# A two-layer mixer and expert kernel: a third expert unit loaded ahead, requests in slot order, late norm rows, residual and gate products at other places of the PE stream

## The reference, cut to what matters

```python
h = _layernorm(DEEPNORM_ALPHA * h + mix, ln_mix_g[layer], ln_mix_b[layer])
ffn = _moe(h, w_router, b_router, moe_w_gate[layer], moe_w_up[layer], moe_w_down[layer])
h = _layernorm(DEEPNORM_ALPHA * h + ffn, ln_ffn_g[layer], ln_ffn_b[layer])
...
for e in range(N_EXPERTS):                       # inside _moe
    h = jax.nn.silu(xt @ w_gate[e]) * (xt @ w_up[e])
    y = y + combine[:, e:e + 1] * (h @ w_down[e]).astype(jnp.float32)
```

## Time and profile before

| | |
|---|---|
| median of 3 runs | 1013.69 us (1008.77 to 1015.44) |
| the profiled execution | 1008.44 us, its span 1006.5 us |
| PE busy | 959.6 us, 95% of the span |
| DVE, ACT, POOL busy | 298.7, 224.0, 15.2 us |
| DMA | 278.84 MB, mean 277 GB/s |
| experts of layer 0, of layer 1 | about 283 to 500 us, about 781 to 998 us |

### The profile page before, as it was taken

The page is one execution under the profiler, slowest core; times in us unless marked ns, Lnnn a source line. Parts: engine busy times, 40 slices in busy tenths (PEclk is TensorE's granted clock), DMA queues, the critical chain, the costliest instruction groups (busy, mean ns, idle before and its releaser), DMA issues.

```text
span 1006.5 us, 9999 instructions
## 1 busy us (share of the span) xinstructions
PE 959.6 (95%) x3984; PEld 512.8 (51%) x3984; DVE 298.7 (30%) x773; ACT 224.0 (22%) x466; POOL 15.2 (2%) x29
## 2 busy tenths in 40 slices
PE   8989999999999999989899999999998999999986
PEld 7644875554543335333385557888445334453321
DVE  4230162331521213120234433564316112121203
ACT  1120243221211112110211533431532111111101
POOL 2000000000000000000000000000000000000001
PEclk9999999999999999999999999999999999999999
DMA  8982424152789999999994423352555899999994
GB/s 274 335 316 85 160 92 167 43 209 83 302 327 388 422 421 421 421 419 422 398 386 143 168 84 124 127 210 82 210 209 218 323 406 421 421 421 421 418 419 165
DMA packets 65779, 278.84 MB, mean 277 GB/s; under 512 B 8852, under 2 KB 9216, under 8 KB 41920
## 3 DMA queue, kind: packets, MB, share of 16 engines
q1 hardware_dynamic: 63856, 271.60, 68.5%
q0 software_dynamic: 1872, 6.53, 1.9%
HBM read 277.04 MB, written 1.06 MB: 276 GB/s over the span
## 4 chain that ended last, share of the span: by engine, by line
PE 83%; DMA 11%; DVE 4%; ACT 1%; issue 1%; SPq 0%; DVEq 0%
PE bank L679 78%; DMA ring<-in_moe_w_up 10%; PE bank L1040 2%; DMA ring<-in_w_in_ab 1%; PE bank L1097 1%; PE bank L1045 1%; PE bank L1393 1%; PE bank L775 1%; ACT feat L1461 0%; PE bank L956 0%; DVE stat L2241 0%; ACT rstd L1461 0%; DVE feat L2223 0%; DVE hT L2248 0%; DVE h L2478 0%
## 5 line engine op out<-in xcount | busy, mean ns | idle before, releaser
L679 PE MATMUL bank<-ring,hT 128*64 128x512 f32 (+1 forms) x832 | 276.7, 597 | 8.9 <-DMA ring<-in_moe_w_up 4.1
L679 PE MATMUL bank<-ring,feat 128*64 128x512 f32 (+1 forms) x1152 | 226.3, 594 | 8.6 <-ACT feat L1461 4.1
L679 PEld LDWEIGHTS bank<-ring,hT 128*64 128x64 f32 (+1 forms) x832 | 109.8, 162 | 165.8 <-issue 157.8
L679 PE MATMUL bank<-hT,ring 128*128 128x256 f32 x768 | 168.4, 380 | 1.2 <-DMA ring<-in_w_in_ab 1.0
L679 PEld LDWEIGHTS bank<-hT,ring 128*128 128x128 f32 x768 | 145.8, 191 | 21.2 <-DMA ring<-in_w_in_ab 1.7
L679 PEld LDWEIGHTS bank<-ring,feat 128*64 128x64 f32 (+1 forms) x1152 | 74.3, 131 | 150.2 <-issue 140.8
L1461 ACT ACTIVATE feat<-bank 32x512 f32<-32x512 f32 (+3 forms) x128 | 61.1, 494 | 393.3 <-PE bank L679 251.3
L679 PE MATMUL bank<-ring,yT 128*128 128x512 f32 x256 | 112.8, 595 | 0.0
L2231 DVE COPY feat<-bank 32x512 f32<-32x512 f32 (+1 forms) x56 | 38.5, 687 | 150.4 <-PE bank L679 149.8
L679 PEld LDWEIGHTS bank<-ring,yT 128*128 128x128 f32 x256 | 47.8, 190 | 55.5 <-issue 54.6
L2223 DVE TENSOR_TENSOR feat<-feat,bank 128x512 f32<-128x512 f32 x16 | 11.0, 688 | 185.7 <-PE bank L679 185.7
(11 more groups left out here) (249 smaller groups left out, 549.9 us busy)
## 6 DMA issues: line engine op xcount, KB each, us to landing
ring<-in_moe_w_up SPq DMA_DIRECT2D x64, 1024.0 KB, 16.4
ring<-in_moe_w_gate SPq DMA_DIRECT2D x56, 1024.0 KB, 14.4
ring<-in_moe_w_down SPq DMA_DIRECT2D x56, 1024.0 KB, 13.0
ring<-in_w_in_ab SPq DMA_DIRECT2D x24, 1024.0 KB, 9.1
ring<-in_w_in_cd SPq DMA_DIRECT2D x24, 1024.0 KB, 12.7
ring<-in_w_out_ab SPq DMA_DIRECT2D x8, 1024.0 KB, 5.8
ring<-in_moe_w_down SPq DMA_DIRECT2D x16, 512.0 KB, 17.9
ring<-in_w_out_cd SPq DMA_DIRECT2D x8, 1024.0 KB, 6.1
```

The lines of the kernel that those rows point to most:

```text
L679: return nc.tensor.matmul(o, l, r, start=start, stop=stop)
```

## The change

1. **A third unit of pair 3 is loaded ahead**: up of its first expert. Its first half goes to `spare`, a tile that now holds `prob` and `gate_row`; its second half to `tok[:, 2]`, where the norm rows lie.
2. **The norm rows are loaded later**: for the norm after layer 0's experts POOL asks for them when the four result banks are done, for the last norm when up of layer 1's pair 3 is done. Before, both were asked for when h was normed after the mixer. DVE applies gain and bias to `h` (now `gained`) after its copies of cd0 and ahead of those of cd1.
3. **Requests in slot order**: SP asks for gate of pair 4 before up and down of pair 3. The skipped units leave slots that gate of pair 4 takes.
4. **Residual products** (`carry`) of token block 0 stand in routing, around `ranks` of block 1; those of block 1 in the two gaps of pair 7. The scatter of quad 0 into block 1's banks now starts the accumulation.
5. **Gate products**: gate uses bank 1. In pairs 0 and 1 the first chunk of the next pair's gate stands ahead of `hid_turn` and the second behind it (`AHEAD`), 4 of 16 products each time.
6. `weights_turn` stands between gate and up, into bank 2.
7. Of the eight pulls before pair 4, the last two now stand between chunks of pair 4's gate, as they do in pair 0.

```diff
@@ build @@
+AHEAD = (1, 2)
...
-        prob = sb("prob", [P, 2, CAUSAL])
-        gate_row = sb("gate_row", [16, 5, SEQ])
+        spare = sb("spare", [P, KC * FF // 2])
...
-        early = ((as_unit(yT[:, 0:8, :]), as_unit(yT[:, 8:16, :])), (as_unit(tok[:, 0, :, :]), as_unit(tok[:, 3, :, :])))
+        early = ((as_unit(yT[:, 0:8, :]), as_unit(yT[:, 8:16, :])), (as_unit(tok[:, 0, :, :]), as_unit(tok[:, 3, :, :])),
+                 (spare[:, :].rearrange("p (k n) -> p k n", n=FF), as_unit(tok[:, 2, :, :])))
...
-        first_pulls = ((0, 1, 0, 1), (2, 3, 0, 1))
+        first_pulls = ((0, 2, 0, 2), (1, 3, 0, 2))
+        second_pulls = ((0, 1, 2, 3), (1, 0, 2, 3))
@@ SP @@
                 fetch_early(1, 1)
+                fetch_early(2, 0)
...
                 fetch_early(0, 1)
-                for i in range(1, PAIRS - 1):
-                    stream_pair(i)
+                sp.wait_ge(h_ready, TB * (2 * layer + 1))
+                fetch_early(2, 1)
+                order = [(i, j) for i in range(1, PAIRS - 1) for j in (0, 2, 4)]
+                order.remove((EARLY_PAIR + 1, 0))
+                order.insert(order.index((EARLY_PAIR, 2)), (EARLY_PAIR + 1, 0))
+                for i, j in order:
+                    stream_part(i, j)
@@ POOL @@
-                if n % 2:
-                    pool.wait_ge(h_ready, TB * n)
+                if n == 1:
+                    for k in plan["ffn0"]:
+                        wait_ready(pool, "ffn0", k)
+                elif n == 3:
+                    wait_ready(pool, f"up1_{EARLY_PAIR // 2}{EARLY_PAIR % 2}", 3)
@@ PE, second_lists @@
                 pull(layer, 0, 0, 3)
+                carry(layer, 0, 0)
                 ranks(layer, 1)
+                carry(layer, 0, 1)
@@ PE, experts @@
+                def gate_chunks(at, ks):
+                    i, pair = divmod(at, 2)
+                    if ks[0] == 0:
+                        claim(f"gate{layer}_{i}{pair}", 1)
+                        held_w[at] = [weights(at, e, KC) for e in range(2)]
+                    for k in ks:
+                        for e in range(2):
+                            last = mm(bank[1][e * 2 * SLOTS:(e + 1) * 2 * SLOTS, :],
+                                      slots_of(xg[i % 2][:, k, :], pair, e), held_w[at][e](k), k == 0, k == KC - 1)
...
-                        for t in range(TB):
-                            for j in range(4):
-                                pull(layer, 1, t, j)
+                        for t, j in ((0, 0), (0, 1), (0, 2), (0, 3), (1, 0), (1, 1)):
+                            pull(layer, 1, t, j)
...
+                            gate_chunks(at, range(2 if at in AHEAD else 0, KC))
+                        if pair:
+                            claim(f"weigh{layer}_{i}", 2)
+                            pe.wait_ge(selw_ready, QUADS * layer + i + 1)
+                            weights_turn(2).then_inc(ready[2], 1)
...
-                        if i == 0:
-                            carry(pair, 0)
+                        if at + 1 in AHEAD:
+                            gate_chunks(at + 1, (0,))
+                        if at == PAIRS - 1:
+                            carry(layer, 1, 0)
                         claim(f"hid{layer}_{i}{pair}", 0)
                         wait_stored(pe, f"up{layer}_{i}{pair}", 3)
                         hid_turn().then_inc(ready[0], 1)
...
-                        if i == 0:
-                            carry(pair, 1)
+                        if at + 1 in AHEAD:
+                            gate_chunks(at + 1, (1,))
+                        if at == PAIRS - 1:
+                            carry(layer, 1, 1)
@@ DVE @@
             for u, first in ((0, 0), (1, 4)):
+                if u:
+                    gained()
```

More of the change, by code:

```diff
@@ L464, in freed @@
                 return half_used, 2 * (PAIRS * layer + i) + j // 2 + 1
-            name, b = ("gate", 2) if j < 2 else ("up", 3) if j < 4 else ("down", 3)
+            name, b = ("gate", 1) if j < 2 else ("up", 3) if j < 4 else ("down", 3)
             return ready[b], plan[f"{name}{layer}_{i // 2}{i % 2}"][b] + 1
@@ L551, in _, with stream_two @@
                         (down, 1, FF // P))
-                def stream_two(n, k, src, half):
+                def stream_two(n, k, src, half, es=range(2)):
                     rows = slice(half * k // 2, (half + 1) * k // 2)
-                    for e in range(2):
+                    for e in es:
                         sp.wait_ge(*freed(n + e - RING, half))
@@ L559, in stream_two, with stream_part @@
                             .then_inc((ring_full, ring_rest)[half][(n + e) % RING], 16)
[L561 to L572, removed]
+                def stream_part(i, j):
+                    src, _, k = pair[j]
+                    if i == PAIRS - 1 and j == 4:
+                        for c in range(k):
+                            for e in range(2):
+                                n = n0 + 6 * i + j + e
+                                sp.wait_ge(*freed(n - RING))
+                                sp.dma_start(slot(n, k)[:, c, :], src[layer, 2 * i + e, :, c, :]) \
+                                    .then_inc(last_in[c], 16)
+                        return
+                    es = [e for e in range(2) if i != EARLY_PAIR or j + e >= EARLY]
+                    for half in range(2):
+                        stream_two(n0 + 6 * i + j, k, src[layer, 2 * i:2 * i + 2], half, es)
                 def fetch_early(j, half):
@@ L578, in fetch_early @@
                         .then_inc(early_in, 16)
-                src_of_early = [gate[layer, 2 * EARLY_PAIR + e] for e in range(EARLY)]
+                src_of_early = [pair[j][0][layer, 2 * EARLY_PAIR + pair[j][1]] for j in range(EARLY)]
                 y_last = ("y_ret3", "y_ssd3")[layer]
@@ L991, in pull, with carry @@
                 last.then_inc(ready[b], 1)
+            def carry(layer, t, q):
+                if t == 0:
+                    claim(f"ffn{layer}", 4 + q)
+                nc.tensor.matmul(bank[4 + 2 * t + q][:, :], residual, h[:, t, q * 512:(q + 1) * 512],
+                                 start=t == 0, stop=False, skip_group_check=True)
             def second_lists(layer):
@@ L1122, in spread_out @@
                         wait_stored(pe, f"down{layer}_{i}{pair}", 2 + q)
-                    wait_stored(pe, f"weigh{layer}_{i}", 1)
-                    last = scatter(t, q)
+                    wait_stored(pe, f"weigh{layer}_{i}", 2)
+                    if i == 0 and t == 1:
+                        claim(f"ffn{layer}", 6 + q)
+                    last = scatter(t, q, start=i == 0 and t == 1)
                     if i == QUADS - 1:
@@ L1145, in experts @@
                         rows = lambda k, e: slots_of(xg[i % 2][:, k, :], pair, e)
[L1146 to L1151 removed]
+                        if at in (0, PAIRS // 2):
+                            first_gate(at)
+                        else:
+                            gate_chunks(at, range(2 if at in AHEAD else 0, KC))
+                        if pair:
+                            claim(f"weigh{layer}_{i}", 2)
+                            pe.wait_ge(selw_ready, QUADS * layer + i + 1)
+                            weights_turn(2).then_inc(ready[2], 1)
                         claim(f"up{layer}_{i}{pair}", 3)
```

96 lines of the change are left out of this document (41 added, 55 removed).

## The result

The changed kernel took **1013.95 us** (median of 20 runs, 1009.64 to 1018.43), the kernel before, run beside it, 1010.52 us (20 runs): ratio 1.0029, 95% interval 1.0017 to 1.0041. The forecast was 6.6 us faster; by the ratio it became 2.9 us slower. That lies within 1%, but on the wrong side, and 1013.95 is above the range. The profiled execution took 1013.29 us, its span is 1011.2 us. Ratios use fast runs alone, and two runs of this study, one of the kernel before (1442.98 us) and one of e2 (1690.01 us), were slow and stand in none.

The account below looks back on a forecast made before the run. The full DMA load stream in both layers' experts was taken as the bound. Layer 0 gains 4.4 us (ring), layer 1 2.5 (bytes), less 0.3 in pair 7: 6.6 off 1013.69 gives 1007.1 us, range 998.5 to 1012.8.

Parts of the forecast that it names:

- g: Time by which PE comes earlier to down of pair 4: -0.1 us in layer 0, -0.4 in layer 1.
- The pulls before pair 4: Idle of 1.39 us ahead of pair 4's gate goes, save some 0.2: PE gains 1.2 us.
- the smaller of x and lead + g: Rule for each layer's gain in the experts: 4.4 us in layer 0, 2.5 in layer 1.
- x: Time by which the experts' load stream runs earlier: 6.2 us in layer 0, 2.5 in layer 1.
- lead: Time queued loads still cover when down of pair 5 is requested: 4.5 us in layer 0, 3.9 in layer 1.
- Third unit, landing without a loss: Its 5.0 us leave the full stretch; its halves load where the queue has room, and SP's wait costs nothing.
- Slot order at 0: Gate of pair 4 requested earlier fills a 3 us hole; pair 3's up and down land later, at no cost.
- Residual products in routing: They fit the idle around `ranks`; in layer 0 the clock stays high, saving 1.2 us.
- Late norm rows: Layer 0's are hidden; layer 1's cost 2.5 us in the full stretch, bounds 0 and 6.6.
- The rival "more": Both layers bound by bytes alone, pair 2's gate landing in time: 10.9 us faster, 1002.8 us; chance 0.20.
- "The clock stays low" as a rival: Low clock after layer 0's routing, plus norm rows at their upper bound: only 1.3 us faster, 1012.4 us; chance 0.28.
- The rival "slower": A longer wait in pair 1 for pair 2's gate delays down of pair 4: up to 1022.0 us; chance 0.06.

Follow-up runs that it names:

- e2: Changed kernel plus ten useless products ahead of pair 2's first gate chunk in pair 1's gap, so PE works while waiting; 1010.33 us, ratio 0.9996.
- e1: Changed kernel without pair 2's gate products in pair 1's gaps (AHEAD = (1,)); 1007.52 us, ratio 0.9965 to the kernel before.
- e3: Kernel before with only the load changes: third unit, slot order, late norm rows, no PE moves; 1009.19 us, ratio 0.9976.
- g2: Changed kernel with pair 2 instead of pair 3 loaded ahead (EARLY_PAIR = 2), so its gate weights are there in time; 1002.20 us, ratio 0.9912.
- f3: e1 with block 1's two residual products moved back from pair 7 to pair 1's gaps; 1006.60 us, ratio 0.9957.
- f2: Kernel before with the PE moves alone, without pair 2's gate products; two early units, old request order, early norm rows; 1009.49 us, ratio 0.9968.
- f1: e1 with SP's requests in the old order, gate of pair 4 behind down of pair 3; 1009.86 us, ratio 0.9984.
- f4: f3 with the last norm rows asked for later, behind up of layer 1's pair 7; 1006.59 us, ratio 0.9950.
- g1: e1 with PE waiting in pair 1 for pair 2's first gate halves, without doing products there; 1015.89 us, ratio 1.0042.

## Why the prediction was wrong

**The step that failed: g, the time that PE is earlier or later at down of pair 4, given as -0.1 and -0.4 us.** Measured from `ranks` to the request for down of pair 5: before 416.17 - 277.20 = 138.97 and 914.03 - 776.53 = 137.50; after 420.64 - 278.87 = 141.77 and 922.06 - 779.52 = 142.54. So g was **-2.8 and -5.0**. The wait itself was computed nearly right (6.3 and 4.7; measured 5.12 and 5.55). What was left out is the clock that falls behind a wait of 5 us. The pieces of the error:

- From the wait's end to pair 2's remaining gate products, 339.50 - 327.19 = 12.3 us passed in layer 0; the prediction's pieces give 0.9 + 1.4 + 6.9 = 9.2. In layer 1, 839.22 - 828.27 = 10.95. That is 3.1 and 1.8 us more; against the 9.46 that e2 took at full clock, **2.9 and 1.5 us** of it are the clock's. The prediction had the very mechanism in front of it, idle and then 0.50 in the earlier trace rows, and used it only where it gave a gain. The Trainium skill (TensorE: Matmul & The Clock Gate, What's actually happening) states it in general: the throttled state is the default and activity releases it. This wait and its two levels agree.
- In layer 1 the load came 1.0 us later than computed. The prediction took 13.2 us from the earlier trace rows for the second gate unit, but that row is the median of two requests (`DMA to landing us min/median/max: 12.1/13.2/14.2`). The second landed 14.2 us after 811.1, at 825.3 and not 824.3. In layer 0, against `ranks`, it came 0.9 us earlier than computed.
- The pulls before pair 4 saved 0.4, not 1.2: from down 3's end to gate 4's end 409.41 - 386.43 = 22.98 against 404.94 - 381.56 = 23.38. Between chunks of gate a four-instruction pull takes 1.26 us (887.21 to 888.47 in e1) where it takes 1.0 in a row.
- Layer 1 lost 1.7 us more in pair 3: its down took 8.78 for 7.09, at a clock of 0.71 in 880 to 885 us, behind an idle time of 0.95 + 0.69. `weights_turn` had left that gap, which held 0.57 + 0.69 in the kernel before. I had priced that move at its duration alone, +0.4. That the wider gap is the cause isn't shown: in layer 0 of the same trace it left the clock alone. Over all profiles a stretch at 0.50 follows this gap in pairs 3 and 5 in 8 of 40 places where it holds 0.95, and in none of 16 where it holds 0.57.

**The rule came near, and always gave too much**, "the smaller of x and lead + g". With the measured g it gives 4.5 - 2.8 = 1.7 and 3.9 - 5.0 = -1.1; T shrank by 0.3 and grew by 1.8. In e1 lead + g is 4.8 and 2.1; measured 3.5 and 1.3. In e3 lead + g is 3.2 and -1.3; measured 1.8 and -1.9. In every kernel whose request for down of pair 5 meets an idle queue, T gains 0.6 to 1.5 us a layer less than the rule says, where the prediction took off 0.15. In g2, requests at 133.72 from `ranks` in both layers make g 5.2 and 3.8, lead + g 9.7 and 7.7, so the bytes decide: 6.2 and 2.5. Measured: 5.8 and 3.0.

**There is a second bound that I missed.** Loads alone can give a layer no more than what PE loses to the stream. I summed 4.9 us in the earlier trace rows, with 1.91 of "issue". That idle time stands ahead of pair 6's gate in every kernel here, 1.6 to 2.7 us in either layer, whatever the loads did. In the source PE there branches on the value that decides on further passes; no run took the branch out. It isn't the stream's, so about 3.0 of the 4.9 were. The changed kernel is limited by PE: after pair 1 it waits for loads for 0.8 us in layer 0 and not at all in layer 1.

Point by point, the rest:

- The starting point was high: the forecast took its 6.6 us off a median of 3 runs, 1013.69 us; 20 runs have 1010.52.
- What the profile was to show: the wait in pair 1, the clock of 1.00 after `ranks`, latencies near 5 us for down of pair 5 and a hole there came. The landing of pair 7's up did not: 0.4 us earlier and 1.7 later, for 4 and 2.5 earlier. Two of the signs that the forecast is wrong came as well: holes elsewhere, near 387 and 398 us (the one at 420 us is also wider than the 2 us forecast, share 0.70 over 5 us), and in layer 1 PE runs through pair 7 without a wait for loads.
- Third unit, landing without a loss: right. Slot order at 0: not quite. Down of pair 3 in layer 0 of e1 and f3 takes 8.2 us where f2 has 7.09, at a clock of 1.00 (e1) and with its last half landing at 377.3 us, in its midst. The 8.8 us in layer 1 of both is the clock's (0.50). The old order was no better by the medians (f1).
- Residual products in routing: right, clock included (1.2 us). In pair 7: right, 490.16 - 487.63 = 2.53 us.
- Late norm rows: layer 0's hidden, right; layer 1's worth nothing with a hole behind them (f4), and 2.5 where none follows only by the reading of f1.
- The rival "more" needed pair 2's gate to be there when PE comes. It was not, but g2 makes it so, and takes 1002.20 us where that rival had 1002.8 (by the ratio it is 8.9 us faster than before, where the rival had 10.9).
- "The clock stays low" as a rival named the clock in the wrong place, behind `ranks`, where it was 1.00, and with g = -1.3 less than half of what came. The rival "slower" named this wait and its path through down of pair 4, and wanted it 4 us longer than computed. The idle was not longer; with the clock and the rest PE was 2.7 and 4.6 us later than computed. A chance of 0.06 was too little for a mechanism whose decision point lay 4 us off, beside a wait of 5.

What stays open: the third unit's share with PE on time (e1 against f2: 0.9997 by the ratios, but 4.6 us of T); why the same idle time is followed by a low clock in one execution and not in another; and what makes the rule give 0.6 to 1.5 us too much.

## What to carry to other kernels

Work moved forward into a gap must have its operands there: count from the load's landing to the gap before moving it, and move the load, not the work, as g2 does. A wait on PE costs its idle time and the low clock behind it, here 1.5 to 2.9 us more on 5. And what a stream runs ahead of its ring gives nothing: before bytes are taken out, sum what the waiting engine really loses to loads, leaving out waits of other kinds.

## What the runs showed of the hardware

- After 5.1 to 5.6 us of idle on PE the granted clock was 0.50 and stayed there into the work that followed, for 6.2 and 3.4 us in the changed kernel and for some 5.7 and 6.9 in g1 (layers 0 and 1). That cost 2.9, 1.5, 2.3 and 2.9 us.
- A low clock can also follow much shorter idle times: 0.95 + 0.69 us ahead of down of pair 1 (e1, 8.78 for 7.09), while the same gap in the same kernel's layer 1 left the clock alone (819.51, 7.09). Of the six such gaps in pair 1 (e1, f1, f2) three were followed by it. With that gap filled, as in f3 and g2, down of pair 1 took 7.0 to 7.1 us in all 14 places.
- One idle time of 2.25 us between the layers was followed by a clock of 1.00 (f2), by a stretch at 0.50 (before), and by a longer one (changed kernel): 278.5, 280.2 and 281.8 us for the same mixer.
- A 1.05 MB load on an idle queue landed after 4.6 to 5.1 us in every kernel, so here this latency showed a hole without a look at the engines' share.
